# A streaming-encoder layer on eight cores: the sample rows computed beside the first prompt tile instead of as a tile of their own

## What is computed

```python
def _layer(x, conv_prev, mem_k, mem_v, sgu_fn, ...):
    z = x @ w_in                                   # 1024 -> 2560: u | v | B | C | x_in
    u, v, gb, gc, xin = jnp.split(z, ...)
    v = _layernorm(v.reshape(bsz, s, 4, 128), ...)
    a_out = sgu_fn(u, v, w_s, b_s)                 # masked 128x128 position mixing, times u
    cx = gc * xin
    cat = jnp.concatenate([conv_prev, cx], axis=1)
    conv = cat[:, 0:s] * w_conv[0] + cat[:, 1:s+1] * w_conv[1] + cat[:, 2:s+2] * w_conv[2]
    mix = jnp.concatenate([a_out, gb * conv], axis=-1) @ w_out
    x = _layernorm(ALPHA * x + mix, ...)
    q = (x @ w_q).reshape(bsz, s, 4, 256)
    p = softmax(einsum('bshd,bmhd->bhsm', q, mem_k) / 16)
    o = einsum('bhsm,bmhd->bshd', p, mem_v)        # 256 memory tokens
    x = _layernorm(ALPHA * x + o @ w_mem_o, ...)
    f = (silu(x @ w_gate) * (x @ w_up)) @ w_down   # 1024 -> 2816 -> 1024
    return _layernorm(ALPHA * x + f, ...)
```

## Time and profile before

| | us |
|---|---|
| three runs: lowest, median, highest | 3859.4, 4004.49, 4190.73 |
| the profiled execution, its own time | 3856.87 |
| its span on the slowest core (of 3826.7 to 3855.1) | 3855.1 |
| PE busy (share of the span) | 3236.8 (84%) |
| DVE, ACT, POOL busy | 2655.3 (69%), 1496.5 (39%), 1710.3 (44%) |
| moved by DMA | 911.65 MB, mean 236 GB/s |

### The profile page before, as it was taken

How to read it: one execution, slowest core, us unless ns; L and a number is a source line. 1 busy time by engine, 2 the same in 40 slices (tenths; PEclk the granted TensorE clock), 3 DMA queues, 4 the chain that set the end, 5 groups by cost and what they waited for, 6 DMA issues and landing times.

```text
span 3855.1 us, 71713 instructions; the slowest of 8 cores (3826.7 to 3855.1 us)
## 1 busy us (share of the span) xinstructions
PE 3236.8 (84%) x21491; PEld 1994.8 (52%) x21491; DVE 2655.3 (69%) x4989; ACT 1496.5 (39%) x2696; POOL 1710.3 (44%) x1386
## 2 busy tenths in 40 slices
PE   4465855398999999999989879999999999999987
PEld 2232533164655556565646436565655556565654
DVE  2447776467777877777776656777777877777764
ACT  2454443133444444443423233343444444443432
POOL 1203344154445464645453353454445453645454
PEclk8687977699999999999989989999999999999998
DMA  9888977886868686868679956686768686868666
GB/s 242 258 257 232 275 216 211 243 280 203 257 206 252 206 274 209 261 203 257 211 251 326 303 164 216 213 258 214 256 204 256 214 265 209 261 202 261 199 217 216
DMA packets 370486, 911.65 MB, mean 236 GB/s; under 512 B 37807, under 2 KB 146095, under 8 KB 370110
## 3 DMA queue, kind: packets, MB, share of 16 engines
q1 hardware_dynamic: 360814, 890.16, 72.5%
q0 software_dynamic: 9296, 16.91, 3.0%
HBM read 837.60 MB, written 86.26 MB: 240 GB/s over the span
## 4 chain that ended last, share of the span: by engine, by line
PE 57%; DVE 12%; DMA 11%; issue 8%; POOL 5%; ACT 4%; SPq 3%; DVEq 0%; POOLq 0%; ACTq 0%
PE bank L1160 21%; PE bank L901 9%; PE bank L1230 9%; PE bank L984 8%; PE bank L1064 4%; DVE x L886 3%; POOL xres L880 3%; PE bank L632 2%; PE bank L939 2%; DMA x<-x_prompt 2%; POOL xres L888 1%; DVE sg L1112 1%; DMA stg<-w_gate 1%; ACT xres L878 1%; DVE stl L863 1%
## 5 line engine op out<-in xcount | busy, mean ns | idle before, releaser
L1116 POOL TENSOR_TENSOR hT<-snap,sg 128x512 f16<-128x512 f32 (+1 forms) x288 | 347.5, 1210 | 531.3 <-DVE sg L1112 463.7
L888 POOL TENSOR_TENSOR xres<-xres,lnb 128x1024 f32<-128x1024 f32 (+1 forms) x195 | 478.9, 2459 | 152.5 <-DVE x L886 126.3
L901 PE MATMUL bank<-mring,mixT 128*128 128x512 bf16 (+1 forms) x2096 | 518.6, 382 | 18.8 <-DVE mixT L1032 10.8
L880 POOL TENSOR_TENSOR xres<-xres,lng 128x1024 f32<-128x1024 f32 (+1 forms) x195 | 463.6, 2386 | 152.5 <-ACT xres L878 152.5
L1166 ACT ACTIVATE snap<-bank 128x512 f32<-128x512 f32 (+1 forms) x576 | 320.4, 562 | 442.4 <-PE bank L1160 414.9
L984 PE MATMUL bank<-xT,mring 128*128 128x512 bf16 (+1 forms) x2176 | 488.4, 369 | 3.6 <-DVE mixT L1029 1.1
L1160 PE MATMUL bank<-x2T,fring 128*128 128x256 f16 x3360 | 440.6, 282 | 52.0 <-DMA fring<-wscS 22.3
L1171 DVE TENSOR_TENSOR snap<-bank,snap 128x512 f32<-128x512 f32 (+1 forms) x576 | 362.5, 640 | 174.3 <-ACT snap L1166 106.2
L878 ACT ACTIVATE xres<-xres,mvl 128x1024 f32<-128x1024 f32 (+1 forms) x195 | 237.1, 1238 | 533.9 <-DVE mvl L876 500.1
L1160 PEld LDWEIGHTS bank<-x2T,fring 128*128 128x128 f16 x3360 | 336.4, 101 | 142.1 <-issue 59.6
L1230 PE MATMUL bank<-fring,hT 128*128 128x512 f16 x1268 | 309.2, 387 | 64.4 <-DMA fring<-wscD 60.2
(11 more groups left out here) (172 smaller groups left out, 4856.4 us busy)
## 6 DMA issues: line engine op xcount, KB each, us to landing
mring<-wscM SPq DMA_DIRECT2D x368, 512.0 KB, 5.5
fring<-wscG SPq DMA_DIRECT2D x347, 512.0 KB, 5.3
stg<-wscG SPq DMA_DIRECT2D x233, 512.0 KB, 5.1
fring<-wscD SPq DMA_DIRECT2D x138, 512.0 KB, 4.8
stg<-wscD SPq DMA_DIRECT2D x94, 512.0 KB, 4.9
xres<-x_prompt SPq DMA_DIRECT2D x64, 512.0 KB, 6.5
y_prompt<-xres SPq DMA_DIRECT2D x64, 512.0 KB, 6.2
fring<-wscD SPq DMA_DIRECT2D x69, 384.0 KB, 4.3
```

Source lines behind the costliest of these rows:

```text
L880: op("gpsimd", lambda e: e.tensor_tensor(out=xv, in0=xv, in1=lng[li][0:SP, :], op=ALU.mult), c_pool(1024), reads=bx + bufs("lng%d" % li), ...
L888: op("gpsimd", lambda e: e.tensor_tensor(out=xv, in0=xv, in1=lnb[li][0:SP, :], op=ALU.add), c_pool(1024), reads=bx + bufs("lnb%d" % li), w ...
L901: r = e.matmul(bk(L)[0:SP, :], lhsT=lhs(j, k0 + k), rhs=t[:, k * 512:(k + 1) * 512], start=(j == 0 and k == 0), stop=(j == cnt - 1 and k = ...
L1116: op(eng, lambda e: e.tensor_tensor(out=dst, in0=Cu().rearrange("p (f t) -> p f t", f=n), in1=g.rearrange("p (f t) -> p f t", f=n), op=ALU ...
```

## The change

The sample position is gone: `tiles` are the 16 prompt tiles. The sample rows have a context of their own, `CS`, whose buffers (residual, transposed rows, mixed rows, hidden rows) are views into slots 2, 3 and 4 of `mring`. `mixer` is split in two: `front(c)`, a generator that asks for its weight pieces and yields, and `attention(c)`. `co_run` drives the fronts of tile 0 and of the sample rows together, so both use a piece while it is in its slot. The sample's attention is done inside `memory()`: for sets 1 and 2 the folded pieces are used directly from the two `pc` buffers and are no longer stored or loaded. The sample's FFN products are issued in `ffn` of tile 0 on the pieces that are there. Until tile 1's mixer has been recorded `mload` uses two slots (`NM[0]`), then five as before. The piece b of each m is now asked for together with x, ahead of the work between them.

The planner changes too: no FFN bank before the last M lease of `memory()` (`fhold`), no M limit but seven banks before `mfree`, up to seven F banks during tile 0's FFN (`fbig`), 0.6 us instead of 1.4 for the power in `ln_tail`, and a span total of 190 instead of 140 for the head. Fifteen small SBUF tensors are now slices of one, `small`; the other edits are names.

```diff
                     first = l.num == head[l.kind]
+                    big = head["F"] < self.fbig
                     if l.kind == "F":
-                        if not first or held["F"] >= 6 or len(avail) - 1 < (1 if ahead else 0):
+                        if not first or held["F"] >= (7 if big else 6) or len(avail) - 1 < (1 if ahead else 0) or head["M"] < self.fhold:
                             continue
-                    elif held["M"] + (1 if first else 2) > 5 or len(avail) - (1 if first else 2) < max(0, 4 - held["F"]):
+                    elif l.num >= self.mfree:
+                        if held["M"] + (1 if first else 2) > 5 or len(avail) - (1 if first else 2) < max(0, (6 if big else 4) - held["F"]):
+                            continue
+                    elif held["M"] + (1 if first else 2) > 7 or len(avail) < (1 if first else 2):
                         continue
...
-    tiles.insert(NT // 2 if spos is None else spos, NT)
...
+        NM = [2]
...
-            i = mctr[0] % RM
+            i = mctr[0] % NM[0]
...
-            for q in range(3):
...
-                            nme = "%s%d%d_%d" % ("ag"[w], n, kh, q)
-                            ld(lambda e, pi=pi, nme=nme: e.dma_start(out=wscM[midx[nme]], in_=pc[pi]), bufs("pc%d" % pi),
-                               bufs("W" + nme), "pc%d" % pi, 524288)
...
+            for w in range(2):
+                for n in range(2):
+                    for kh in range(2):
+                        ap, b = fold(w, n, kh)
+                        nme = "%s%d%d" % ("ag"[w], n, kh)
+                        ld(lambda e, ap=ap, nme=nme: e.dma_start(out=wscM[midx[nme]], in_=ap), [b], bufs("W" + nme),
+                           "pc%d" % ((pctr[0] - 1) % 2), 524288)
+
+            for q in (1, 2):
+                load_kv(q, 0)
+                for n in range(2):
+                    pa = [fold(0, n, kh) for kh in range(2)]
+                    L = lease("M")
+                    for j in range(2):
+                        def f(e, L=L, j=j, pa=pa):
+                            for k in range(4):
+                                r = e.matmul(bk(L)[0:64, :], lhsT=CS.xT[:, j * 4 + k, 0:64], rhs=pa[j][0][:, k * 512:(k + 1) * 512],
+                                             start=(j == 0 and k == 0), stop=(j == 1 and k == 3))
...
+                    softmax(L, 64, q - 1, PTs[q - 1][:, n * 4:(n + 1) * 4, :], [buf("mxS_%d_%d" % (n * 4 + k, q - 1)) for k in range(4)])
...
+        CS.xr, CS.xrn = mring[2][:].bitcast(F32).rearrange("p (s d) -> p s d", s=1), "xrS"
+        m3 = mring[3][:]
...
+        m4 = mring[4][:].bitcast(FP16)
...
-            op("gpsimd", lambda e: e.tensor_tensor(out=m[0:SP, s, 3:4], in0=m[0:SP, s, 2:3], in1=mhalf[0:SP, 0:1], op=ALU.pow), 1.4,
+            op("gpsimd", lambda e: e.tensor_tensor(out=m[0:SP, i, 3:4], in0=m[0:SP, i, 2:3], in1=mhalf[0:SP, 0:1], op=ALU.pow), 0.6,
...
-                px, bpx = mload("x%d" % m)
+                ((px, bpx), (pb, bpb)) = yield ["x%d" % m, "b%d" % m]
...
-                pb, bpb = mload("b%d" % m)
...
+        def co_run(gens):
+            want = [next(g) for g in gens]
+            while want[0] is not None:
+                got = [mload(n) for n in want[0]]
+                assert all(w == want[0] for w in want)
+                want = [next_or_none(g, got) for g in gens]
...
+                    if cs is not None and i in rhs_s:
+                        if i == 1:
+                            bank["s"] = lease("F")
+                        Rs, rsn, half = rhs_s[i]
...
+                                        r = e.matmul(bk(L)[:, c0:c0 + 64], lhsT=ft[:, o:o + 128], rhs=Rs[:, k, :],
+                                                     start=(i == 1 and mat == 0 and fi == 0 and k == 0), stop=(k == 3), skip_group_check=True)
...
+                                    r = e.matmul(bk(L)[0:64, :], lhsT=hS[:, F * 11 + cg * 4 + k, :], rhs=ft[:, k * 512:(k + 1) * 512],
+                                                 start=(i == 1 and cg == 0 and k == 0), stop=(cg == 2 and k == nc_ - 1), skip_group_check=True)
...
-        span(-2.6, 2.3, 140.0)
-        mixer(0, memory)
+        span(-2.6, 2.3, 190.0)
+        C = [ctx(p) for p in range(NPOS)]
+        co_run([front(C[0]), front(CS)])
+        memory()
+        S.fhold = nleases["M"]
+        attention(C[0])
+        S.mfree = nleases["M"]
...
+            ffn(C[pos], CS if pos == 0 else None)
...
+                NM[0] = RM
+                mctr[0] = 0
```

549 lines of the change are left out of this document (286 added, 263 removed).

## The result

The changed kernel took 3877.88 us (median of 5 runs, 3876.55 to 3880.66), the kernel before 3859.4 us beside it; the ratio is 1.0057, with a 95% interval of 1.0039 to 1.0075. A second group of runs gave 1.0068 (1.0041 to 1.0094). So it is slower by half a per cent, clear of the intervals though far under 2%, where 3764 us, 2.4% less, was forecast. Its time lies inside the range, but no rival described it.

The account below looks back on a forecast made before the run. It took the head to be paced by DMA and weight preparation, the rest by TensorE. Terms -117 + 28 + 8 + 10 - 4 - 20 + 10 - 8 = -93 against 3856.87 us gave 3764 us, range 3700 to 3910.

Parts of the forecast that it names:

- Term 6: Seam of two steady tiles: cheaper power price reorders it, saving half a microsecond per tile, 15 times, -8 us (bounds +-27).
- The forecast's own test: Sign of failure: the last preparation unit comes after 790 us or the steady tile period moves by over 2 us.
- Terms 4 and 5c: Two ring slots: tile 0's front waits for landing stores, +10 us; loads for tile 1's mixer and tile 0's attention, +10.
- the 135 named: Sign in tile 0's front: the slot cost there is wrong if the last front store leaves much after 135 us.
- its check: Sign in the head: the estimate for two-slot loads is wrong if SP's waits for TensorE double.
- Terms 5a and 5b: Weight preparation in the head: earlier start behind fewer stores, -4 us; faster pace from 12.6 MB less traffic, -20 us.
- the check of 5b: Sign in the preparation: the faster pace is wrong if units keep 7.2 us each.
- Term 3: End of tile 0: 39 uncovered sample down-projection matmuls cost +8 us (bounds +4, +12); other sample matmuls cost nothing under idle time.
- Term 2: Tile 1: less of tile 2's mixer runs ahead, 40 matmuls instead of 192, +28 us (bounds +23 and +33).
- Term 1: Middle of the kernel: the sample position disappears with its 34 MB of loads, -117 us (bounds -113 to -120).
- The chance of 0.05 for slower: Probability of a slower result; its rival (0.04) had mring loads holding SP for their whole landing, 3988 us.
- the gap of 81 ns: Skill's rule for weight load and matmul pairs of 128 columns; would make 480 sample matmuls 39 us instead of 14.

Follow-up runs that it names:

- after_again: The changed kernel unaltered, run again on another chip beside the kernel before: mean span +26.8 us against the kernel before, ratio 1.0068.
- a_price14_again: Repeat run of the changed kernel with only the planner's power price set back from 0.6 to 1.4 us: -54.1 us against the kernel before, ratio 0.9837.
- a_nosample: Changed kernel with power priced at 1.4 us and all the sample rows' own work left out: -106.9 us against the kernel before, ratio 0.9714.

## Why the prediction was wrong, by its own steps

- **Term 6, the steady tiles (-8), is the step that failed**: it measured +81 (after_again against a_price14_again, 66 in the kernel before). It had the pieces: the order with the transpose moved ahead, 8 us for the load, "its transpose is also asked for earlier". It priced the gain (the wait that the matmuls fill) and not the wait that takes its place. Counting forward from the load would have given it: between the load at 1635.47 and the transpose TensorE had work only until 1640.1, 4.7 us against a landing near 8, some 3 us per seam. The rest of the 6 to 7 us came behind it: the waits for snap and Tb, and the lower clock. Its bound of 1.8 us either way came from the waits of before; a reordered wait isn't bounded by the wait that it replaces. The forecast's own test, the period moving by over 2 us, says so.
- **Terms 4 and 5c, the slots (+20)** measured +39 in the kernel before. The median landing fell as assumed (11.8 to 9.1 us), but the last store left at 145.9, past the 135 named: the front's chain became cast, store, landing, next cast. The doubled waits of SP for TensorE didn't come: up to 800 us they are 75 us in all against 100 before, none of a group over 13.6. (The 26.2 us of the earlier trace rows were the groups of L984 alone; with L901, L939 and L1064, which read mring too, they were 46.6.) 5c cost through something else than its check looked for, and what that is no run shows.
- **Terms 5a and 5b (-24).** By the check of 5b (units at 7.2 us; they took 497.9 / 70 = 7.1) it was wrong. SP waited even longer for GpSimd's copies, as against the earlier trace rows:

```profile
SPq L302 <- POOL stg L844: 213.4, 55, 13.4
```

  Yet the sum wants such a gain. The distance of a_nosample, less what its tiles 1 to 15 differ from those of before (-124, parts as in the first table), leaves +17 for the end of tile 0, where two slots alone cost some 39: fewer bytes and stores gave back about 22. That is worked out over three chips, not shown.
- **Term 3 (+8)** measured 9.4 at the end of tile 0, in one execution, and 2.6 in the whole. But that the sample's other work goes "under the 205 us in which TensorE is idle" at a price of nothing was wrong: for a_price14_again the same reckoning leaves +34, so by this reckoning across chips the sample rows' own work costs 17 us ahead of that end, front and down projection together.
- **Term 2 (+28)** measured +22.6, near its lower bound (+23), and for the reason that the order showed; the cause of that order, the slots, wasn't named.
- **Term 1 (-117)** measured -112.5 by the distance and -114.7 by the tiles.

With these sizes, of which the 22 and the 17 are worked out and not measured: -113 + 23 (tile 1) + 34 (39 - 22 + 17, the end of tile 0) + 81 = +25, against +26.4. Of the miss of about 119 us, 89 are term 6 and 30 the head. The chance of 0.05 for slower sat on one mechanism, waiting mring loads, and none on the seams, though the seam was the one place where the order was seen to change for all tiles.

Of the two rules of the Trainium skill that the prediction weighed, the trace does not bear out the gap of 81 ns even at 128 columns: the eight transposes at 1643.31 us, a weight load each, started 55 ns apart, as did those at 2709.80 in the kernel before, and the measurement decides. The estimate of 3.2 us for a 512 KB DMA stands against 9.1 us, again under load, and the front was not free at it.

## What to carry to other kernels

A planner's cost is one of a set of numbers that are wrong together. Make one true alone and the order moves by the errors of the others, once per tile; set the price and the landing that it is weighed against in one edit, or look at the first wait of the new order. When a wait in an in-order queue is moved, count what the queue has to do between the issue of the load and the instruction that needs it, and multiply by the number of tiles before pricing anything that happens once. And ring slots that are lent to other data can cost in three places, of which the runs price the first and the third and not the second by itself: where stores must land before a slot is used again, where loads wait for readers, and where the next user finds its slot taken.
